# Four raw places and four pairs of split halves, in place of six and three, in a four-layer decoder trunk

## The reference

```python
h = x
for i in range(DEPTH):              # 4
    kind = i % 3                    # attention, S5, pooling, attention
    m = mixer[kind](h)
    h = layer_norm(DN_ALPHA * h + m, ln_g[i, 0], ln_b[i, 0])
    h = layer_norm(DN_ALPHA * h + swiglu(h, ffn_w1[i], ffn_w3[i], ffn_w2[i]),
                   ln_g[i, 1], ln_b[i, 1])

def swiglu(x, w1, w3, w2):          # 1024 -> 2816 -> 1024
    return (jax.nn.silu(x @ w1) * (x @ w3)) @ w2
```

## Time and profile before

| | us |
|---|---|
| median of 3 runs | 1381.52 |
| lowest, highest | 1376.92, 1382.16 |
| the profiled execution | 1377.7 |
| its span, first to last instruction | 1375.9 |
| TensorE busy | 1253.1 |
| VectorE busy | 871.3 |
| ScalarE busy | 608.8 |
| GpSimd busy | 158.8 |

### The profile page before, as it was taken

The page is one execution under the profiler, slowest core; times in us unless marked ns, Lnnn a source line. Parts: engine busy times, 40 slices in busy tenths (PEclk is TensorE's granted clock), DMA queues, the critical chain, the costliest instruction groups (busy, mean ns, idle before and its releaser), DMA issues.

```text
span 1375.9 us, 20817 instructions
## 1 busy us (share of the span) xinstructions
PE 1253.1 (91%) x8432; PEld 1123.8 (82%) x8432; DVE 871.3 (63%) x1286; ACT 608.8 (44%) x939; POOL 158.8 (12%) x206
## 2 busy tenths in 40 slices
PE   5998899899986899899998878999989988999996
PEld 3886699889966677899997868999977986899996
DVE  5775879999571524655556966555567764655556
ACT  3365355444442033544444445444445553544442
POOL 1540009930090000000000000000001000000000
PEclk9997899999985679899999898999999998899998
DMA  9542356445474224365554444655544333465551
GB/s 368 158 150 77 122 169 202 136 157 187 164 190 123 77 92 153 126 217 189 188 185 150 142 153 125 217 189 189 186 151 162 132 108 107 138 217 189 188 187 46
DMA packets 62353, 220.35 MB, mean 160 GB/s; under 512 B 7985, under 2 KB 9777, under 8 KB 61489
## 3 DMA queue, kind: packets, MB, share of 16 engines
q1 hardware_dynamic: 55890, 202.50, 44.7%
q0 software_dynamic: 5504, 14.95, 3.7%
q10 hardware_dynamic: 864, 1.57, 0.4%
HBM read 210.34 MB, written 7.60 MB: 158 GB/s over the span
## 4 chain that ended last, share of the span: by engine, by line
PE 78%; DVE 15%; ACT 3%; issue 3%; DMA 1%; SPq 0%; DVEq 0%; ACTq 0%
PE bank L1158 15%; PE bank L1160 14%; PE bank L1159 14%; PE bank L1169 9%; PE bank L1171 9%; PE bank L1173 8%; DVE wlo L674 4%; PE bank L1391 2%; DVE stats L687 1%; DVE slot L686 1%; PE bank L1321 1%; ACT whi L423 1%; PE bank L1334 1%; PE bank L1343 1%; DVE slot L752 1%
## 5 line engine op out<-in xcount | busy, mean ns | idle before, releaser
L674 DVE TENSOR_TENSOR wlo<-raw,whi 128x1024 fp32r<-128x1024 f32 x370 | 462.2, 1251 | 326.5 <-ACT whi L423 325.1
L423 ACT ACTIVATE whi<-raw 128x1024 fp32r<-128x1024 f32 x370 | 391.5, 1059 | 489.2 <-PE bank L1160 271.0
L1158 PE MATMUL bank<-xhi,whi 128*128 128x256 f32 x1728 | 498.4, 288 | 15.2 <-DVE xlo L743 9.3
L1159 PE MATMUL bank<-xlo,whi 128*128 128x256 f32 x1728 | 494.4, 286 | 0.0
L1160 PE MATMUL bank<-xhi,wlo 128*128 128x256 f32 x1728 | 494.1, 286 | 0.0
L1158 PEld LDWEIGHTS bank<-xhi,whi 128*128 128x128 f32 x1728 | 336.9, 195 | 23.8 <-issue 13.0
L1159 PEld LDWEIGHTS bank<-xlo,whi 128*128 128x128 f32 x1728 | 337.2, 195 | 2.9
L1160 PEld LDWEIGHTS bank<-xhi,wlo 128*128 128x128 f32 x1728 | 337.0, 195 | 0.0
L1169 PE MATMUL bank<-whi,hhi 128*128 128x512 f32 x320 | 100.3, 395 | 1.8 <-DVE wlo L674 1.8
L1173 PE MATMUL bank<-whi,hlo 128*128 128x512 f32 x320 | 99.7, 393 | 0.0
L1171 PE MATMUL bank<-wlo,hhi 128*128 128x512 f32 x320 | 99.6, 392 | 0.0
(11 more groups left out here) (282 smaller groups left out, 1462.6 us busy)
## 6 DMA issues: line engine op xcount, KB each, us to landing
raw<-in_w SPq DMA_DIRECT2D x370, 512.0 KB, 3.4
slot<-in_ln_row POOLq DMA_DIRECT2D x16, 512.0 KB, 5.4
toep<-slot POOLq DMA_DIRECT2D x8, 512.0 KB, 15.7
toepA<-toep SPq DMA_DIRECT2D x2, 1024.0 KB, 10.2
BT<-toep SPq DMA_DIRECT2D x2, 1024.0 KB, 4.9
x_tm<-in_x SPq DMA_DIRECT2D x1, 1024.0 KB, 5.0
slot<-in_s_B SPq DMA_DIRECT2D x1, 1024.0 KB, 16.9
slot<-in_s_C SPq DMA_DIRECT2D x1, 1024.0 KB, 19.0
```

The lines of the kernel that those rows point to most:

```text
L423: nc.scalar.activation(whi[:, c % SPL, :], raw[:, c % RAW, :], ACT.Copy).then_inc(w_hi, 1)
L674: V.tensor_tensor(wlo[:, c % SPL, :], raw[:, c % RAW, :], whi[:, c % SPL, :].bitcast(F32), ALU.subtract).then_inc(w_lo, 1)
L1158: mm(dst, wh, bhi[:, kc, :], start=(i == 0), stop=False)
L1159: mm(dst, wh, blo[:, kc, :], start=False, stop=False)
```

## The change

Two sizes change. The buffer raw has four places in place of six, and whi and wlo have four places each in place of three: 6 + 3 + 3 and 4 + 4 + 4 tiles of 4 KB per partition, the same space.

```diff
-RAW = 6
-SPL = 3
+RAW = 4
+SPL = 4
```

## The result

The changed kernel takes 1367.19 us in the median (1364.4 to 1370.23, 5 runs) beside 1381.52 us before (1376.92 to 1382.16, 5 runs). The ratio is 0.990, with a 95% interval of 0.988 to 0.9921: 14.3 us or 1.0% less. The forecast was 1375.0 us, 6.5 us less, in a range of 1368.5 to 1381. The time lies just under that range.

What follows compares the result with a forecast made beforehand. TensorE, busy 91% of the span, was taken as the bound. Gains of 4.5 + 1.0 + 0.4 + 0.6 = 6.5 us gave 1375.0 us against the 1381.5 median, range 1368.5 to 1381.

Steps and rivals of the forecast that it cites:

- The reading of what bounds the kernel: Whole kernel: TensorE is busy 91% of the span; split waits fall on engines that mostly have time.
- S5 hand-over: Before the S5 recurrence: tile 107 splits sooner, so u's copies and transfers finish earlier; 4.5 us less, bounds 2.9 and 6.6.
- the whole stretch: S5 work from 427.6 to 495.9, mean granted clock 0.62: expected to start sooner but last as long.
- Rival (b): S5 work: shorter idle time brings the full clock back sooner, 5 us more gain, 1370.0 us; 14%.
- Mixer ends: Two attention layers and the pooling layer: the first residual step no longer waits behind a split; 0.4 us for three.
- Table stretch: First feed-forward stage, 246.8 to 290: VectorE enters it sooner; 1.0 us less, between 0 and 2.
- The start: First tiles: less load traffic lets GpSimd's copy start sooner; 0.6 us gain, between a 1.7 loss and a 2.6 gain.
- spread of 3 us: Allowance around the forecast for the bounds, granted-clock steps after each norm, and runs of before differing by 5 us.
- The signs to look for: Changed profile: sooner splits and S5 copies, L1379 near 8 us, unchanged total split waits, 3.4 us landings, no later raw waits.
- Rival (a): S5 transfers are bound by something that doesn't move, such as GpSimd's stores; only 2.0 us gained, 1379.5 us; 17%.
- (c): Feed-forward stages: four raw places run short when landings last over 9.1 us; slower, 1409 us; 4%.

Runs made afterwards that it cites:

- the first profile: The changed kernel's first profiled execution, 1364.4 us, set beside a profiled execution of the kernel before, 1377.7 us.
- the second pair: Two later profiled executions without further edits: the kernel before at 1381.87 us and the changed kernel at 1367.36 us.
- the last experiment: Both kernels executed twice more, unchanged: 1381.87 and 1379.38 us for the kernel before, 1364.93 and 1367.36 us for the changed one.
- upper group: Runs of the unchanged kernel before whose times gather near 1382 us.
- lower group: Runs of the unchanged kernel before whose times gather near 1378 us.
- the S5 experiment: Changed kernel with the four-tile split distance for tiles 105 to 107 alone, three for all others: 1370.89 us, ratio 0.9924 to the kernel before.

## Why the prediction was wrong

**The reading of what bounds the kernel** held. The waits of ScalarE and VectorE at splits lost 540 us and TensorE's waits for low halves 0.6.

**S5 hand-over, 4.5 us.** The mechanism was right to the instruction: split, first copy, issues. The idle time fell by 3.9 us (12.6 to 8.8), between the bounds of 2.9 and 6.6. The term was 0.6 too large because the landings follow each other by 1.07 us, where one per 1.0 was taken, and the last one waits for its turn. The Trainium skill (DMA: Bandwidth & Descriptors, "Issuing engines are not separate DMA queues") says that transfers of all issuing engines run on the same 16 DMA engines and interleave. The spacing of 1.07 us agrees; that this would push the term to its lower bound of 2.9, as the prediction had it, did not come true.

**The step that failed: "I expect the whole stretch to move without shrinking."** It was wrong by 2.7 us in seven of the nine profiles with the short idle time. Rival (b) said that the clock would come back some microseconds sooner if the idle time were shorter; it was given 14%, on the ground that the low level had long outlasted the idle time. The earlier trace rows show one stretch with a mean clock of 0.62, and I read it as one low stretch followed by work that doesn't depend on it. It had in fact several steps in it (full clock from 467.0 to 480.7 and from 487.5 to 490.9), and a mean cannot show that some of them stand only a few microseconds from the next one. (b)'s 1370.0 us was the nearest of the four.

**Mixer ends, 0.4 us for three: mis-sized.** I costed the split that stands ahead of the residual step (its end against its bank's) and took what stood in the earlier trace rows, the last attention. At the first one L950 to L952 stand between the two, 1.9 us on VectorE. It gave 2.0 to 2.1 us at the norm, of which 0.9 went at the two tiles behind it, which ran longer at the low clock. The other two ends gave 0.2 us each at the norm, and half or more of it went at the tiles behind. The mistake is to have taken one end's rows for all three: the list ahead of each residual step had to be read.

**Table stretch, 1.0 us:** 1.4, of which 1.1 is the wait at tile 64 that is gone. The rule in the Trainium skill (SBUF — State Buffer, "Who interferes with whom"), by which a VectorE instruction with two SBUF inputs contends with a GpSimd instruction that reads SBUF, would have left it near 0. The trace shows the contention, though mostly elsewhere: before's low half of 4.3 us, which the prediction names, stands beside GpSimd's copy in the last attention, at 1053.2, and the longest in the table stretch take 2.1 to 3.0 us. It does not show that VectorE's head start is taken back.

**The start, 0.6 us:** 0.8 and 0.4, but by another way than the one described. The loads were as late as worked out (tile 4 landed at 24.8, sooner than 28.5, tile 5 2.5 us behind it), and the copy was released sooner, as said. I had its effect on tile 5, whose wait of 2.62 us fell to nothing in the first profile and to 1.80 in the second pair; I had not seen that the copy could fall on a low half, which cost tile 3 3.2 us in the first. Whether it does is a matter of 0.4 us, as the last experiment shows.

**What was left out altogether: the granted clock in layer 0.** 0 to 3.1 us at tiles 13 to 15, 0 to 1.7 at tile 24, 0.7 to 0.8 until tile 99. The forecast put that into its spread of 3 us, as something that averages out. It does not: the median of before lies in its upper group, and the change leaves that group empty. This is also why the forecast against the median was hard. It subtracted from the median what it had worked out on an execution of the lower group, and so treated 3.8 us as scatter that the change would keep. Left out as well were 0.6 us of idle time at tiles 13 to 15.

The clock behind the S5 idle time and the clock in layer 0 are most of the miss. With the 2.7 us of the first the forecast would have been 1372.3 us, and with the 3.1 us of the second pair at tiles 13 to 15 1369.2, both inside the range; the first norm, the table stretch, the wait at L1321 and what comes until tile 99 make up the rest.

**The signs to look for.** Right: split 107 right behind 106, the first copy (4.0 us before the product's end), the wait at L1379 near 8 us (8.8), tile 5. Wrong: ScalarE was to wait for no raw tile after the start, and did once in the first profile (3.2 us) and three times in that of 1367.36 (6.7 us), in the last attention; TensorE's only wait for a low half there is the 1.0 us at tile 275 that before has too. Wrong too: ScalarE's wait for TensorE at the splits was to stay as long in total and fell from 484 to 145 us. With four places the limit of its splits is their own position in the list, behind silu and hhi, not the place. The raw landings were 3.8 us in the median, not 3.4. That goes with the sooner wait and not with the four places: 3.3 to 3.5 us in all profiles with the old wait in most places, with six places or four, and 3.7 to 4.0 with the sooner one and at least three places. Why was not tested.

**Rival (a)** is excluded by the S5 experiment, **(c)** by the ones with three and two places.

What stays open: why the granted clock takes one course or another in executions of the same kernel with the same idle times, so that two kernels with the short idle time still had a read-out of 14.1 us; and which part of the start keeps the entry of the attention at the full clock.

## What to carry to other kernels

- Ask what stands in an engine's list behind a wait for a buffer, and whether somebody on the bound needs it. Three tiles of 370 carried 6.7 us; a reordering of two lines gave the same step in its profile with the old buffers. Read the list ahead of each such place, not of one of a kind.
- Where the bounding engine idles and then runs at its low clock, idle time can cost more than its length: 3.9 us less idling took 6.6 us off in seven profiles of nine. Forecast such a place as two numbers, and look at the steps of the clock, not at its mean.
- Loads need only as many places as a landing and the place's own use last, over the bound's time per tile: three were enough here, two cost 69 us against four (with five pairs of halves).

## What the hardware showed that was not expected

- GpSimd's copy of 16 x 4096 took 3.6 to 4.5 us wherever it was put, and stretched the VectorE instruction that ran beside it: a low half from 1.2 to 4.50 us, and L902, of 128 x 64, from 0.2 to 3.62 us. At three positions it cost TensorE 2.6 to 3.2 us; at the start of the constants, from 7.57 us on, the wait for the input was no longer than without it (4.65 and 4.84 us).
- Executions of one kernel differ by 4 us, 3.1 of them through the granted clock at one place, while TensorE's waits at tiles 3 and 5 before it agree within 0.1 us.
- Eight transfers of 128 KB from SBUF to SBUF, of two issuing engines, land one after the other, 1.07 us apart on average, 4.1 to 6.3 us after SyncE's issues.
